# A two-layer decoder step on one core: the query chunk as seven block products, with more sums on GpSimd and a new order on VectorE and ScalarE

## What is computed

```python
h = rmsnorm(x, g_mix_pre[l])
qa, ka, va, qi, ki, wi, qb, kb, vb, gb = project_mixers(h, w_in[l], pos)   # one h @ w_in, then rotary positions
a = mixer_a(qa, ka, va, qi, ki, wi)            # sparse attention over the keys that an indexer picks
b, S = retention_mixer(qb, kb, vb, gb, s0, g_ret[l])
x = x + rmsnorm(concat([a, b]) @ w_out[l], g_mix_post[l])
f = square(relu(rmsnorm(x, g_ffn_pre[l]) @ w_up[l])) @ w_down[l]
x = x + rmsnorm(f, g_ffn_post[l])

# indexer, for each query t and key s
sc[t, s] = sum_h wi[t, h] * relu(qi[t, h] . ki[s])      # s <= t
sel      = top_k(sc[t], 128)                             # 64 for the samples
```

## Time and profile before

| | us |
|---|---|
| median of three timed runs | 1561.29 |
| lowest, highest | 1555.24, 1561.61 |
| the profiled execution | 1559.19 |
| its span, first to last instruction | 1557.4 |
| TensorE busy | 1538.7 (99%) |
| VectorE busy | 828.6 (53%) |
| ScalarE busy | 456.9 (29%) |
| GpSimd busy | 495.0 (32%) |

### The profile page before, as it was taken

How to read it: one execution, slowest core, us unless ns; L and a number is a source line. 1 busy time by engine, 2 the same in 40 slices (tenths; PEclk the granted TensorE clock), 3 DMA queues, 4 the chain that set the end, 5 groups by cost and what they waited for, 6 DMA issues and landing times.

```text
span 1557.4 us, 21913 instructions
## 1 busy us (share of the span) xinstructions
PE 1538.7 (99%) x8054; PEld 1172.1 (75%) x8054; DVE 828.6 (53%) x1698; ACT 456.9 (29%) x1057; POOL 495.0 (32%) x434
## 2 busy tenths in 40 slices
PE   8999999999999999999999999999999999999998
PEld 5445777688888888888844467666888888888887
DVE  4599786847652013333567978859466510133335
ACT  5223356125331003310242224561353210122101
POOL 0006401023653424344310063010246424234461
PEclk9999999999999999999999999999999999999999
DMA  6426311024332122212223262111143321322211
GB/s 202 142 74 217 136 56 55 3 86 135 135 110 95 66 108 82 84 67 93 88 80 109 82 231 95 56 56 41 64 145 132 111 82 57 128 87 82 81 55 55
DMA packets 52812, 150.42 MB, mean 97 GB/s; under 512 B 8250, under 2 KB 29506, under 8 KB 39394
## 3 DMA queue, kind: packets, MB, share of 16 engines
q1 hardware_dynamic: 45778, 140.52, 26.3%
q10 hardware_dynamic: 6928, 8.50, 1.6%
HBM read 139.79 MB, written 9.02 MB: 96 GB/s over the span
## 4 chain that ended last, share of the span: by engine, by line
PE 82%; DVE 14%; ACT 2%; issue 1%; POOL 0%; DMA 0%; ACTq 0%; DVEq 0%; POOLq 0%
PE ps L1217 47%; PE ps L873 9%; PE ps L1155 7%; PE ps L827 7%; DVE arena L1907 3%; DVE top L1905 3%; PE ps L1025 2%; PE ps L1015 2%; PE ps L792 1%; PE ps L1002 1%; DVE x_feat L2056 1%; PE ps L805 1%; PE ps L1113 1%; DVE arena L2133 1%; PE ps L929 1%
## 5 line engine op out<-in xcount | busy, mean ns | idle before, releaser
L1217 PE MATMUL ps<-arena,wring 128*128 128x256 f32 (+1 forms) x1280 | 285.8, 382 | 0.3 <-DVE arena L2140 0.3
L1217 PEld LDWEIGHTS ps<-arena,wring 128*128 128x128 f32 x1280 | 243.0, 190 | 37.7 <-DVE arena L2140 1.1
L827 PE MATMUL ps<-wring,h_feat 128*128 128x512 f32 (+1 forms) x576 | 254.7, 583 | 2.4 <-ACT h_feat L1338 2.3
L2452 POOL TENSOR_TENSOR wring<-wring,arena 128x512 f32<-128x512 f32 (+1 forms) x48 | 78.8, 1642 | 347.0 <-PE ps L1217 323.6
L827 PEld LDWEIGHTS ps<-wring,h_feat 128*128 128x128 f32 x576 | 103.3, 190 | 108.6 <-issue 97.0
L1217 PE MATMUL ps<-h_feat,wring 128*128 128x256 f32 (+1 forms) x768 | 176.6, 381 | 0.0
L1217 PEld LDWEIGHTS ps<-h_feat,wring 128*128 128x128 f32 x768 | 145.9, 190 | 21.6
L1217 PE MATMUL ps<-mix,wring 128*128 128x256 f32 (+1 forms) x512 | 120.2, 383 | 1.5 <-DVE p_sb L2114 1.5
L1217 PE MATMUL ps<-arena 128*128 128x264 f32 x512 | 119.2, 386 | 0.0
L1155 PE MATMUL ps<-mix,wring 128*128 128x256 f32 (+1 forms) x512 | 115.1, 384 | 0.0
L2435 POOL TENSOR_TENSOR pt_sb<-pt_sb 128x256 f32<-128x256 f32 (+1 forms) x94 | 72.6, 773 | 124.8 <-ACT pt_sb L1312 121.9
(11 more groups left out here) (257 smaller groups left out, 2149.6 us busy)
## 6 DMA issues: line engine op xcount, KB each, us to landing
wring<-in_w_all SPq DMA_DIRECT2D x108, 1024.0 KB, 5.1
arena<-in_cache_k SPq DMA_DIRECT2D x32, 256.0 KB, 5.2
arena<-in_cache_v SPq DMA_DIRECT2D x32, 256.0 KB, 4.3
o_k_out<-arena ACTq DMA_DIRECT2D x2, 1024.0 KB
o_v_out<-arena ACTq DMA_DIRECT2D x2, 1024.0 KB
arena<-in_state SPq DMA_DIRECT2D x2, 1024.0 KB, 4.8
o_rets_out<-arena ACTq DMA_DIRECT2D x2, 1024.0 KB, 10.1
wring<-in_w_idx SPq DMA_DIRECT2D x3, 648.0 KB, 4.0
```

Of the source, the lines that this page charges most:

```text
L827: last = mm(ps[:, bank_of(c, i), 0:width], h_feat[:, k, token_cols(t)], wt, start=(k == 0), stop=(k == KD - 1))
L1217: last = mm(out, a[:, j, :], b, start=(opens(n) and j == 0), stop=(j == nk - 1), skip_group_check=True)
L2452: nc.gpsimd.tensor_tensor(dst, in0, in1, op).then_inc(s_ready, 1)
```

## The change

- Chunk 1 is computed by `project_blocks`. It has buffers of its own for two input sums (in `mix`) and two weight sums (in `qT`). `beside_q` is laid out anew: the indexer transposes stand in the third block product of the order (2, 3) and (2, 5), the six pairs of dot products at the places in `DOTS`, the samples' query transposes at (6, 5) instead of in chunk 2, the samples' dot products at (7, 4).
- GpSimd makes four input sums and four weight sums for chunk 1 at the start of each layer. The two that chunks 5 and 6 share with it (in2, in3) are not made again; in1 and in4 are made again as sums 5 and 6. All are in quarters, as before.
- VectorE's order in chunk 1 is new: the tile of samples is rotated within the chunk, tile 2 after the last scores, tiles 3, 0 and 1 after the last product; one round of block 1 stands before and one after the last four `combine`, four behind the rotations.
- Six of block 3's rounds and its mask move between attention steps (`late_rounds`); three instead of nine rounds stand before the sample's maximum.
- ScalarE copies P1 of chunk 4 before the sample's exponentials; the indexer's key stores are issued after the fourth score.
- In layer 1 TensorE computes tiles 2 and 3 of chunk 0 together, one eighth of h after the other; the token scales of the first tiles come after all updates of x instead of after the third.
- In the first eight feed-forward stages the fourth `square_sum` of a stage comes after the `second_sum` two stages on, instead of at the end of the next stage.

```diff
--- before.py
+++ after.py
@@ -51,7 +51,7 @@
 CHUNKS = 8
 CONSTS = 10
 FT = 16
-BLOCKED = (4, 5, 6)
+BLOCKED = (1, 4, 5, 6)
...
@@ -105,6 +105,7 @@
     return (0, 1, 2, 3, 5)[n] if n < TILES else n % 2
 
 
+DOTS = [(3, 2), (4, 0), (4, 6), (5, 4), (6, 2), (7, 0)]
...
@@ -356,7 +357,8 @@
 
         in1, in2, in3, in4 = quarter(gate_flat, 3 * W), quarter(mix_high, 0), quarter(mix_high, 2 * W), quarter(temps, 0)
         gate_tmp = [mix_high[:, t * W:(t + 1) * W] for t in range(NT)]
-        cs1, cs2 = quarter(kbd_flat, 0), quarter(kbd_flat, 2 * W)
+        first_in1, first_in4 = quarter(mix_flat, 0), quarter(mix_flat, 2 * W)
+        first_cs, cs = [[quarter(a, 2 * i * W) for i in range(2)] for a in (qT.rearrange("p h n -> p (h n)"), kbd_flat)]
         raw = [temps[:, i * W:(i + 1) * W] for i in range(3)]
         rt = p_sb
...
         def tokens_of(c):
 
-            return {4: zr[1], 5: zr[0], 6: gate}[c]
+            return {1: zr[1], 4: zr[1], 5: zr[0], 6: gate}[c]
+
+        def sums_of_chunk(c):
+            return first_cs if c == 1 else cs
...
@@ -811,6 +816,9 @@
                 for i, t in enumerate(tile_order(c)):
                     if c == 0 and now[0] == 0 and t < NT:
                         continue
+                    half_here = c == 0 and now[0] and SEQ // 2 // P <= t < NT
+                    if half_here and t > SEQ // 2 // P:
+                        continue
...
+                            if half_here:
+                                if k == KD - 1:
+                                    last.then_inc(proj_done, 1)
+                                last = mm(ps[:, bank_of(c, i + 1), 0:width], h_feat[:, k, token_cols(t + 1)], wt,
+                                          start=(k == 0), stop=(k == KD - 1))
...
-                    if n == 5 and c == 6:
-                        pe.wait_ge(in_sums, past(in_sums) + 4 * 5)
+                    if n == 5 and c == 1:
+                        pe.wait_ge(in_sums, past(in_sums) + 4 * 1)
+                    if n == 5 and c > 1:
+                        pe.wait_ge(in_sums, past(in_sums) + 4 * (7 if c == 6 else 5))
...
-                    if n == 4:
+                    if n == 4 and c == 1:
                         pe.wait_ge(in_sums, past(in_sums) + 4 * 4)
+                    if n == 4 and c > 1:
+                        pe.wait_ge(in_sums, past(in_sums) + 4 * 6)
...
                     if (i, k) == (1, KD - 1):
                         pe.wait_ge(sq_used, past(sq_used) - PER_LAYER["sq_used"] + square_number(now[0] - 1, 5, 0, KD - 1)[1])
                         token_sums(0)
-                    if (i, k) == (3, KD - 1):
+                    if (i, k) == (2, KD - 1):
                         pe.wait_ge(sq_used, past(sq_used) - PER_LAYER["sq_used"] + square_number(now[0] - 1, 5, 1, KD - 1)[1])
                         token_sums(1)
...
             def beside_q(i, k):
-                if (i, k) == (0, KD - 1):
+                if (i, k) == (2, 3):
...
+                if (i, k) == (2, 5):
                     transpose_group(zr[0], 2 * P, 2 * P + HD)
-                if 1 <= i <= 3 and k % 4 == 1:
-                    j = 4 * (i - 1) + k // 2
+                if (i, k) in DOTS:
+                    j = 2 * DOTS.index((i, k))
...
-                if (i, k) == (3, KD - 1):
+                if (i, k) == (6, 5):
+                    pe.wait_ge(rope_done, past(rope_done) + TILES + 1)
+                    pe.wait_ge(ts_read, past(ts_read) + 1)
+                    transpose_sample(zr[1], pairs)
+                if (i, k) == (7, 4):
                     pe.wait_ge(kidx_in, past(kidx_in) + 16 * NB * NPAGES)
-                    pe.wait_ge(ts_read, past(ts_read) + 1)
...
@@ -953,7 +974,6 @@
                     pe.wait_ge(dot_read, past(dot_read) + 3 * NI)
                     transpose_group(zr[1], *pairs[0])
                     transpose_group(zr[1], *pairs[1])
-                    transpose_sample(zr[1], pairs)
...
-                project(1, beside_q)
+                project_blocks(1, beside_q)
...
-                evacuate(1, 0)
+                take_p1(1)
+                evacuate(1, 1)
...
-                act.dma_start(ki_out[bass.ds(l, 1)].rearrange("a (t p) n -> p (a t) n", p=P), zr[0][:, 0:NT, NI * HD:(NI + 1) * HD]).then_inc(out_ki, 16)
-                act.dma_start(kis_out[bass.ds(l, 1)].rearrange("a p n -> (a p) n"), zr[0][0:NB, NT, NI * HD:(NI + 1) * HD]).then_inc(out_ki, 16)
+                take_first(1)
...
-                    if j % 4 == 3:
-                        evacuate(1, 1 + j // 4)
+                    if j == 3:
+                        act.dma_start(ki_out[bass.ds(l, 1)].rearrange("a (t p) n -> p (a t) n", p=P), zr[0][:, 0:NT, NI * HD:(NI + 1) * HD]).then_inc(out_ki, 16)
+                        act.dma_start(kis_out[bass.ds(l, 1)].rearrange("a p n -> (a p) n"), zr[0][0:NB, NT, NI * HD:(NI + 1) * HD]).then_inc(out_ki, 16)
+                    if j == 5:
+                        take_p5(1)
+                    if j == 9:
+                        scale_quad(1, "22", proj_c22)
+                act.wait_ge(ts_mm, past(ts_mm) + 2)
...
+                scale_quad(1, "12", proj_c12)
                 act.wait_ge(sdot_mm, past(sdot_mm) + 1)
                 nc.scalar.activation(rs[:], ps[:, 2:4, 0:L], ACT.Relu).then_inc(srelu_done, 1)
                 act.wait_ge(srelu_done, up(srelu_done))
-                evacuate(1, 4)
+                scale_quad(1, "21", proj_c21)
...
+                take_p1(4)
...
-                take_p1(4)
...
+            late_rounds = [(4, 6, 0), (4, 7, 0), (4, 7, 1), (5, 6, 1), (5, 7, 0), (5, 7, 1)]
...
+                if (c, i, s) in late_rounds:
+                    select_top(sc[3], top8[:], 1)
+                if (c, i, s) == late_rounds[-1]:
+                    block_mask(3)
...
+                combine(0)
+                combine(1)
+                chunk_u2(1)
+                combine(2)
+                combine(3)
+                rope(1, NT)
+                combine(4)
+                combine(5)
+                chunk_u3(1)
+                chunk_c22(1)
+                combine(6)
+                combine(7)
+                select_top(sc[1], top8[:], 1)
+                combine(8)
+                combine(9)
+                chunk_c12(1)
+                combine(10)
+                combine(11)
+                select_top(sc[1], top8[:], 1)
+                rope(1, 2)
+                chunk_c21(1)
+                rope(1, 3)
                 rope(1, 0)
-                for j in range(3 * NI):
-                    combine(j)
-                    if j % 4 == 3:
-                        rope(1, 1 + j // 4)
-                rope(1, 4)
-                select_top(sc[1], top8[:], 6)
+                rope(1, 1)
+                select_top(sc[1], top8[:], 4)
...
-                select_top(sc[3], top8[:], 9)
+                select_top(sc[3], top8[:], 3)
...
                 chunk_u2(4)
-                select_top(sc[3], top8[:], TOPK_P // 8 - 15)
-                block_mask(3)
+                select_top(sc[3], top8[:], TOPK_P // 8 - 9 - len(late_rounds))
...
                 for q in range(EARLY):
                     second_sum(q)
+                    if q > 1:
+                        square_sum(q - 2, 3)
                     if q:
                         square_sum(q - 1, 0)
                         square_sum(q - 1, 1)
@@ -2361,8 +2411,7 @@
                     if q:
                         square_sum(q - 1, 2)
                     take_c12(q)
-                    if q:
-                        square_sum(q - 1, 3)
+                square_sum(EARLY - 2, 3)
...
                 for k in range(KD if l < DEPTH - 1 else 0):
                     update(2, 1, k)
-                    if k == 2:
+                    if k == KD - 1:
                         now[0] = l + 1
                         token_scales(0)
                         now[0] = l
...
-                if n == 4:
+                if n == 6:
                     pool.wait_ge(rope_done, past(rope_done) + 3 * TILES)
                 b11, b12 = h_feat[:, 0:4, low], h_feat[:, 0:4, high]
                 b21, b22 = h_feat[:, 4:8, low], h_feat[:, 4:8, high]
-                if n == 5:
+                if n == 7:
                     pool.wait_ge(cache_used, past(cache_used) + 2 * NB)
-                dst, in0, in1_ = {1: (in1, b12, b11), 2: (in2, b22, in1), 3: (in3, b22, b12), 4: (in4, in2, b21),
-                                  5: (last_in1, b12, b11)}[n]
+                dst, in0, in1_ = {1: (first_in1, b12, b11), 2: (in2, b22, first_in1), 3: (in3, b22, b12), 4: (first_in4, in2, b21),
+                                  5: (in1, b12, b11), 6: (in4, in2, b21), 7: (last_in1, b12, b11)}[n]
...
             def chunk_sum(c, n):
 
-                q = BLOCKED.index(c)
                 if n == 1:
                     for u in (2 * c, 2 * c + 1):
```

(25 more changed lines are left out.)

37 lines of the change are left out of this document (17 added, 20 removed).

## The result

The changed kernel takes 1565.02 us (median of 16 runs, 1562.64 to 1568.79), the kernel before 1559.2 us (16 runs beside them, one a stray of 4113.81 that does not move the median); the ratio is 1.0047, 95% interval 1.0038 to 1.0055. The changed kernel is slower, clear of the noise, by an amount at the edge of the half per cent that the prediction calls no change. The forecast was 1562.2. The profiled execution took 1563.05 us, span 1561.3, 3.9 us over the span before. The mean granted clock is 0.995 in it against 0.998 before; in six of the 16 runs it is 0.993, and these are the six slowest, 1566.6 to 1568.8.

The account below looks back on a forecast made before the run. The prediction took TensorE, busy 78.2 of 79.6 us, to bound the kernel. Layer 0 +2.0, layer 1 +2.5 and feed-forward -1.5 gave +3.0 on 1559.2: 1562.2 us, range 1549.5 to 1570.

Parts of the forecast that it names:

- Products: Query chunk: seven block products of 256-wide instructions replace 512-wide ones, 25.7 against 29.0 us, saving 3.3 us a layer.
- Waits for the rotations beside GpSimd: Indexer transposes: TensorE waits for VectorE rotations slowed by GpSimd's sums, 3.6 us (2.5 to 4.5) and 5.2 us (3 to 6).
- the row's price: Indexer rotations: each VectorE operation takes 0.42 us more beside GpSimd additions, as read from the trace; used for the sum.
- the rule's hardest reading: Indexer rotations: a whole GpSimd addition of 0.73 us stands before each operation, making layer 1 wait 9 us.
- Waits at the key transposes: After the query chunk: VectorE is late with the key rotations, so TensorE waits 2.8 us in both layers; bounds 1.5 and 3.2.
- T + 13.5: After the end of chunk 1 (T): when VectorE begins the first key rotation, 3.45 us later than before.
- Early copy of P1: Chunk 4: copying before the sample's exponentials removes TensorE's wait, -1.4 us in layer 0 and -1.3 in layer 1.
- late rounds: Attention: selection rounds moved between steps make VectorE later there, +0.3 us a layer; bounds 0 and 2.
- Layer 1's first tiles: Start of layer 1: GpSimd's last square comes 1.2 us earlier as token scales leave VectorE's updates, -1.2; bounds -0.5 and -2.
- Feed-forward: Feed-forward part: moving one sum of squares removes TensorE waits of 0.73 and 0.78 us, -1.5; bounds -0.5 and -1.5.
- Clock: Layer 1: the 3.0 us lost to a halved granted clock goes but comes back at the 5.2 us wait, net 0.
- the slow clock after each new wait: Rival: clock falls at up to five new waits, 3.0 us each; four falls give 1571.2 us; chance 0.12.

Follow-up runs that it names:

- sums_for_free: Changed kernel with GpSimd's query-chunk sums over 8 of 256 columns, VectorE's four rounds behind the keys, layer 1's tiles one after the other: 1545.36 us.
- gains_alone: Kernel before with only the early copy of P1 of chunk 4, the six late rounds and the moved sums of squares: 1553.13 us.
- short_sums: Changed kernel with GpSimd's eight query-chunk sums over 8 of 256 columns, so most are not computed: 1557.07 us.
- products_alone: Changed kernel without the early copy of P1 of chunk 4, the late rounds and the moved sums of squares: 1568.31 us.
- tiles_in_turn: Changed kernel with token tiles 2 and 3 of layer 1's first chunk one after the other again: 1563.57 us.
- keys_first: Changed kernel with four selection rounds and block 1's mask moved on VectorE from before the first key rotation to behind the last: 1554.06 us.
- gains_plus: gains_alone with VectorE's token scales of layer 1's first half moved behind the last update: 1551.22 us.
- shifted: keys_first with the indexer's transposes and dot products 2.65 us later, ScalarE's copy of P2 earlier, three more rounds behind the keys: 1551.76 us.
- delay_3: gains_alone with three added MAX8 on VectorE before the last key rotation, in both layers: 1554.60 us.
- p5_first: shifted with layer 1's tiles in turn, P5 ahead of P6, GpSimd's sums in that order, transposes and dot products later, seven rounds behind keys: 1546.30 us.

## Why the prediction held, step by step

The time was right (1562.2 against 1565.0, range 1549.5 to 1570), in part by luck: two steps were off by more than the whole forecast of +3.0, the waits beside GpSimd and the clock, and they cancelled.

- **Products, -3.3 a layer.** Measured -3.4 and -3.5 (sums_for_free against gains_alone). Right.
- **Waits for the rotations beside GpSimd, 3.6 and 5.2.** Measured 1.9, below the stated bound of 2.5, and 3.1. The cause is right (short_sums) and so is the price per operation (0.77 and 0.94 against 0.32 and 0.49, so 0.45). In layer 0 the third sum began at 31.1 and not at 30.5, and the rotations 0.6 us earlier, so six operations were slow and not nine. How much of that TensorE sees hangs on when it starts the chunk: it waits 0.99 us in products_alone (start at 27.64) and 0.62 in tiles_in_turn (27.42). In layer 1 TensorE was not there yet: it had stood 2.9 us for the last square and then run slowly. Where it comes unhindered the wait is 4.77 (tiles_in_turn), near the 5.2 by the row's price and far from the 9 us of the rule's hardest reading.
- **Waits at the key transposes, 2.8 a layer.** Measured 2.99 twice. VectorE began the first key rotation at T + 13.53 in layer 0; the text said T + 13.5. Right, and keys_first shows that with four rounds in another place nothing is waited for.
- **Early copy of P1, -1.4 and -1.3, late rounds +0.3 each.** Both waits are gone; D grew by 0.4 and 0.5. Right. products_alone adds that without the early copy only 0.55 and 0.45 us of the waits would have been left behind the new ones, but with slow clock each: its C is 2.2 us longer than the changed kernel's in both layers.
- **Layer 1's first tiles, -1.2.** F is 1.0 less, with 0.2 of slow clock in it. Right in size and cause, the token scales (gains_plus). The 2.9 us wait for the square was implied ("the token sums behind it wait"), but the wait had no number of its own and its clock was only priced in a rival.
- **Feed-forward, -1.5.** E shrank by 0.2 and 1.0, 1.2 in sum. Both waits of 0.7 are gone, but layer 0 has a new one, for another sum of VectorE:

```profile
440.63 2.05 PE L1237 MATMUL ps<-h_feat,wring 128*128 128x264 f32 x8 [0.52 <-DVE arena L2166]
```

Of the kernels with the moved sum of squares, those with this wait, 0.43 to 0.60 us long, have 369.1 or 369.2 us in E of layer 0, and those without it, such as gains_alone and shifted, 368.36. What brings it in some and not in others stays open.

- **Clock, 0.** This is the mis-sized term. The 3.0 us lost in layer 1 before did go. But four falls came and not one: 1.7 and 1.6 behind the key transposes, 1.6 behind the square, 1.6 behind the first transposes of layer 1. That is 6.5 - 3.0 = +3.5 instead of 0. The rival "the slow clock after each new wait" described what happened; its price was too high for the changed kernel, since it took 3.0 us for a fall from the one example at hand, where these cost 1.6 or 1.7.

So two errors cancelled in the profiled run, which gave +3.9 for the forecast +3.0: 3.8 us too much for the rotations, 3.5 us too little for the clock. The other 1.2 us are a sum of small terms. Not in the forecast are 0.6 for the waits at the transposes, four of them, of which each costs some 0.15 more from start to start than the idle time shown, and 0.3 for the chunk's second weight unit in layer 0 (TensorE waits 0.25 at 30.99, as it comes there 0.5 sooner than forecast). The waits at the keys, the late rounds and the feed-forward part came out higher by 0.4, 0.3 and 0.3, the start and the products lower by 0.6 and 0.3. The rest, 0.2, is within the rounding. The median lies 2 us above the profiled run; how many falls of the clock the other executions had, no profile shows.

## What to carry to other kernels

A saving on the engine that bounds a kernel is worth only what its helpers can follow: before moving work to an idle engine, list for each of its results who waits, and order the consumers by how many of those results they need (P5 ahead of P6, with the transposes moved along, was worth 6 us here). In this kernel a wait of TensorE of 2.5 us at the transposes is to be priced at 4, one of 1.1 us at about itself; but far shorter waits brought the slow clock at other places, so each place has to be looked at. When one wait is removed, look for the second chain that ends at the same point.

## What the runs showed of the hardware

**The granted clock after waits.** In the kernels above TensorE stood 20 times for 2.5 to 4.8 us in front of the transposes, the token sums or P6, and 19 times ran at 1.2 GHz behind it, mostly from 0.4 to 1.7 us behind its end on; the exception is the 3.02 us of short_sums in layer 1. The 4.6 to 4.8 us before the very first product are not counted, and the granted clock was 1.00 behind them. After 1.06 and 1.08 (delay_3), 1.88 (changed kernel) and 2.00 us (keys_first) it kept 2.4 GHz. But it also fell at the wait of 1.3 us in layer 1 before, at 0.45 and 0.55 us in products_alone, and in gains_alone and p5_first at a row of waits under 0.7 us, where 18 instructions took 6.86 us instead of 5.17 (p5_first); in the kernel before, the same row of waits had no fall. In the kernel before, in short_sums (layer 0) and in shifted the clock was low already before the wait ended and stayed low about twice as long; the fall then cost 3.0 and 2.8 us in the first two:

```profile
113.70:120.60 6.90, 5.91 (x16) 3.47 (x17) 6.52 (x17) 1.39 (x3) 0.76 (x4) 0.51 0.01 2
```

What sets these apart was not tested.

**VectorE beside GpSimd.** A rotation operation, with two inputs in SBUF, took 0.40 to 0.45 us more beside GpSimd's additions over 256 columns, and nothing more beside such over 8. One thing was new: the first step of the scores, which reads one tensor and one value a row, grew too, by 0.55. In the changed kernel beside GpSimd, and in sums_for_free with GpSimd idle:

```profile
818.19 0.90 DVE L1919 TENSOR_SCALAR arena<-s_sb,wi 128x256 f32<-128x256 f32 x1 [7.25 <-ACT s_sb L1602]
```

```profile
804.13 0.35 DVE L1912 TENSOR_SCALAR arena<-s_sb,wi 128x256 f32<-128x256 f32 x1 [6.06 <-ACT s_sb L1595]
```

The Trainium skill, "SBUF — State Buffer", section "Who interferes with whom", names this operation among those that can take the ports shared with GpSimd in their two-port modes. The two rows agree; which mode the operation ran in, no row shows.
